# A first feed-forward layer as seven block products in two phases, with activation blocks kept in DRAM

## What is computed

```python
def conv_ffn(h, w_up, conv_w, conv_b, w_down):
    gate, val = jnp.split(dwconv_centred(h @ w_up, conv_w, conv_b), 2, axis=-1)
    return (jax.nn.silu(gate) * val) @ w_down
```

## Time and profile before

| | |
|---|---|
| median of 3 runs | 3455.32 us (3455.08 to 3456.81) |
| span of the profiled execution | 3455.1 us |
| TensorE busy | 3150.0 us, 91% |
| VectorE busy | 2289.4 us, 66% |
| GpSimd busy | 1200.4 us, 35% |
| ScalarE busy | 946.3 us, 27% |
| DMA | 196.12 MB, 57 GB/s on average |

### The profile page before, as it was taken

How to read it: one execution, slowest core, us unless ns; L and a number is a source line. 1 busy time by engine, 2 the same in 40 slices (tenths; PEclk the granted TensorE clock), 3 DMA queues, 4 the chain that set the end, 5 groups by cost and what they waited for, 6 DMA issues and landing times. The chain is left out here.

```text
span 3455.1 us, 53810 instructions
## 1 busy us (share of the span) xinstructions
PE 3150.0 (91%) x19598; PEld 2589.7 (75%) x19598; DVE 2289.4 (66%) x3256; ACT 946.3 (27%) x1512; POOL 1200.4 (35%) x1007
## 2 busy tenths in 40 slices
PE   5999989887889999999998769999998799999998
PEld 3889966665778888888886537777777577877786
DVE  8986067886366666666666436666664677777777
ACT  3111245544121111111110335554542221111111
POOL 1322145551222222222220121222121376777764
PEclk8999999998999999999999869999999899999999
DMA  4558120004011111111100200000002111111111
GB/s 195 195 191 290 68 78 2 2 2 160 31 43 37 42 42 37 36 36 37 42 30 0 83 9 10 6 5 5 5 13 80 31 49 49 55 55 49 50 48 73
DMA packets 64395, 196.12 MB, mean 57 GB/s; under 512 B 7697, under 2 KB 21009, under 8 KB 62993
## 3 DMA queue, kind: packets, MB, share of 16 engines
q1 hardware_dynamic: 47280, 163.63, 14.5%
q10 hardware_dynamic: 16992, 30.83, 2.6%
HBM read 175.56 MB, written 18.87 MB: 56 GB/s over the span
## 5 line engine op out<-in xcount | busy, mean ns | idle before, releaser
L1431 DVE SCALAR_TENSOR_TENSOR resid<-ps,mod,resid 128x256 f32<-128x256 f32 x528 | 342.0, 661 | 259.5 <-PE ps L1327 259.3
L1334 PE MATMUL ps<-hf_hi,up_hi 128*128 128x512 f32 (+1 forms) x1056 | 376.6, 357 | 17.5 <-DVE hf_lo L295 12.8
L1334 PE MATMUL ps<-hf_lo,up_hi 128*128 128x512 f32 (+1 forms) x1056 | 376.6, 357 | 0.0
L1334 PE MATMUL ps<-hf_hi,up_lo 128*128 128x512 f32 (+1 forms) x1056 | 374.8, 355 | 0.0
L1792 DVE SCALAR_TENSOR_TENSOR resid<-ps,mod,resid 128x512 f32<-128x512 f32 x352 | 255.8, 749 | 96.1 <-PE ps L1600 95.6
L1621 PE MATMUL ps<-x_hi,w_spare 128*128 128x512 f32 x824 | 290.3, 395 | 9.9 <-DVE x_lo L1717 9.2
L1302 POOL TENSOR_SCALAR up_hi<-up_raw 128x1024 fp32r<-128x1024 f32 x44 | 46.3, 1053 | 690.0 <-PE ps L1334 655.8
L837 POOL TENSOR_TENSOR k_decayed<-decay,qk 128x256 f32<-128x256 f32 (+1 forms) x240 | 193.2, 833 | 193.3 <-ACT decay L1002 193.3
L131 DVE CUSTOM_DVE_ANT_0 ps<-adaw_ring,cond,adab 128x1024 f32<-128x1024 f32 x128 | 205.8, 1608 | 55.7 <-DMA adaw_ring<-in_adaw 44.9
L1334 PEld LDWEIGHTS ps<-hf_hi,up_hi 128*128 128x128 f32 x1056 | 201.5, 191 | 44.0 <-issue 19.2
L1334 PEld LDWEIGHTS ps<-hf_hi,up_lo 128*128 128x128 f32 x1056 | 200.8, 190 | 28.6
(11 more groups left out here) (320 smaller groups left out, 8582.1 us busy)
## 6 DMA issues: line engine op xcount, KB each, us to landing
up_raw<-in_up SPq DMA_DIRECT2D x88, 512.0 KB, 3.5
adaw_ring<-in_adaw SPq DMA_DIRECT2D x80, 512.0 KB, 4.1
dn_raw<-in_dn SPq DMA_DIRECT2D x44, 512.0 KB, 3.5
vr<-vr_out ACTq DMA_DIRECT2D x80, 128.0 KB, 3.1
adaw_first<-in_adaw SPq DMA_DIRECT2D x16, 512.0 KB, 22.5
wvr_raw<-in_wvr SPq DMA_DIRECT2D x8, 1024.0 KB, 7.2
x<-in_xT ACTq DMA_DIRECT2D x8, 640.0 KB, 17.0
r<-vr ACTq DMA_DIRECT2D x10, 512.0 KB, 3.8
```

The costliest lines, as they stand in the source:

```text
L1334: mm = pe.matmul(c.psf[:, at:at + w], a[:, half, k, :], b[:, k, t:t + w], start=(k == 0 and a is up_hi and b is h_hi), stop=(k == KD - 1 a ...
L1431: dve.scalar_tensor_tensor(resid[:, m, t:t + w], c.ps[:, 6 + j % 2, 0:w], c.mod[:, gate + m, cond[t]:cond[t] + 1], resid[:, m, t:t + w], A ...
```

## The change

`ffn` and `ffn_layer` are removed, and `block_layer` with the new `block_ffn` takes their place for layer 0. With W = 640 (half of the 1280 tokens) it works in two phases.

**Start.** VectorE scales the residual in place in half-token blocks, in two parts where a block holds the 256 context tokens. ScalarE shifts the context part (`shift_context`). Then VectorE forms the differences of blocks, and for each of the seven activation blocks ScalarE writes the high part and VectorE the low part, all kept in SBUF for the phase. As this overwrites the residual, the stage before stores it to DRAM: eight 640 KB DMAs on ScalarE's queue after the squares (`spill`), with a wait for all of them at that stage's end.

**Up phase.** 22 units, one for each hidden tile. A unit is seven products of 4 k-blocks x 3 passes x 640 tokens. A region of 640 columns spans bank borders, so each pass is two matmuls, of 256 and 384 or 320 and 320 columns. Three of the seven go into a region TMP and accumulate there; ScalarE copies it out three times a unit (`move`). VectorE makes five sums of 640 columns a unit, the taps and the product. The finished activation isn't used at once: ScalarE copies it to SBUF (`keep`), VectorE forms block sums for each pair of tiles (`join`), and seven blocks of 128 x 640 for each pair are stored to DRAM.

**Down phase.** Seven products, each summed over 11 pair steps in four PSUM regions of 640 columns (4 output blocks). A step is 4 x 3 x 2 = 24 matmuls of 320 columns. For each step SyncE loads one activation block (320 KB), ScalarE makes high parts of it and of a weight block, VectorE and GpSimd the low parts, and in four of the products GpSimd also forms one weight sum per step. Ring depth is 3. VectorE adds to the residual only after a product's eleventh step (`adds`). The down weights come in four loads of 11 x 512 x 128 fp32 (2.88 MB), and the residual is loaded back, 5.24 MB.

The diff, cut to the parts spoken of (weights are also laid out anew on the host):

```diff
@@ project, ScalarE @@
                         act.activation(sq[:, s, span].unsqueeze(1), x[:, bass.ds(m, 1), span],
                                        ACT.Square).then_inc(squared, 1)
+                        if spill is not None:
+                            act.dma_start(spill[:, bass.ds(m, 1), :], x[:, bass.ds(m, 1), span]
+                                          ).then_inc(spilled, 16)
+                if spill is not None:
+                    act.wait_ge(spilled, 16 * tiles)
@@ ffn and ffn_layer @@
-def ffn(c, block, layer, h_hi, h_lo, resid, groups, seqs, wup_d, conv_d, wdn_d, out_d, ready):
...
@@ block_ffn (new) @@
+PAIRS = FT // 2
+RING = 3
+PRODUCTS = (0, 1, 2, 4, 3, 5, 6)
+DOWN = (1, 6, 0, 2, 3, 4, 5)
+TO = (("11",), ("21",), ("11",), ("21",), ("22",), ("12",), ("21", "22"))
...
+    G0, V0, TMP = (128, 1664, 3264) if W == 640 else (0, 1024, 2048)
...
+    place = (TMP, G0, TMP, G0 + W, TMP, V0 + W, V0)
+    home = [1024 * q + 192 if W == 640 else (4 + q) * BANK for q in range(HK)]
...
+    @block.sync
...
+        sp.wait_ge(block_out[1], 16 * PAIRS)
+        up_done(0)
+        for k in range(RING):
+            load(0, k, k)
+        up_done(2)
+        load_weights("12", a12, 0, 1)
+        up_done(4)
+        load_weights("22", a22, 1, 1)
+        up_done(5)
+        load_weights("11", a11, 0, 0)
+        for k in range(KD):
+            up_done(5 if k < HK else 6)
+            sp.dma_start(resid[:, k, span], spill_d[:, k, :]).then_inc(resid_in[k], 16)
+        store_value(LAST, 1, PAIRS - 1)
+        store_joined(1, PAIRS - 1)
+        for k in range(RING, PAIRS):
+            if k == 6:
+                for q in range(7):
+                    sp.wait_ge(block_out[q], 16 * PAIRS + 16)
+                load_weights("21", a21, 1, 0)
+            sp.wait_ge(d_split, k - 2)
+            load(0, k, k % RING)
...
+    @block.tensor
...
+                if pos == 1 and s:
+                    pe.wait_ge(gate_read, f * ns)
+                if pos == 2:
+                    pe.wait_ge(moved, f * 3 + 1)
+                if pos == 3 and W == 640:
+                    pe.wait_ge(mixed, f * sums_n + 1)
+                if pos == 4:
+                    pe.wait_ge(moved, f * 3 + 2)
+                if pos == 5:
+                    if s:
+                        pe.wait_ge(kept, f)
+                        pe.wait_ge(joined, f * 2 + (4 if s % 2 == 0 else 3))
...
+                for turn in ([[q] for q in spans] if pos >= 5 else [spans]):
+                    if pos == 6 and turn[0][0]:
+                        pe.wait_ge(mixed, f * sums_n + 4)
+                    for k in range(HK):
+                        if s == 0:
+                            pe.wait_ge(x_split, pos * HK + k + 1)
+                        for a, b in split_passes(w_hi[ring], w_lo[ring], x_hi[name], x_lo[name]):
+                            for at, m in turn:
+                                mm = pe.matmul(c.psf[:, place[pos] + at:place[pos] + at + m], a[:, k, :],
...
+        if W == 640:
+            for k in range(RING):
+                ready(k)
+                run(0, k, k, k, (0, 3), k == 0, False)
+            pe.wait_ge(kept, FT)
+            pe.wait_ge(joined, 4 * PAIRS + 4)
+            for k in range(RING):
+                run(0, k, k, k, (1, 2), k == 0, False).then_inc(product_done, 1)
...
+    @block.scalar
...
+        def body(act, f, s, pair):
+            if s:
+                centre_value(f - 1)
+                move(f, ua, 0)
+                keep(f - 1, (s - 1) % 2, pair)
+                move(f, ub, 2)
+            round_raw(f, s, 6)
+            act.wait_ge(mixed, f * sums_n + 1)
+            move(f, ua, 4)
...
+        for k in range(KD):
+            if ns > 1:
+                if k + 1 < KD:
+                    shift_context(k + 1)
+                act.wait_ge(shifted, k + 1)
...
+            high(k // HK, k % HK, b11 if k < HK else b21, shift_of(k))
...
+    @block.vector
...
+        def body(dve, f, s, pair):
+            if s:
+                first_value(f - 1)
+                taps(f - 1, 1)
+                product(f - 1)
+                first_gate(f)
+                join(f - 1, (s - 1) % 2, pair)
+            second_gate(f)
+            for part in range(len(value_parts) - 1):
+                second_value(f, part)
+            taps(f, 0)
+            second_value(f, len(value_parts) - 1)
...
+        dve.wait_ge(w_split, UPS)
+        for k in range(2):
+            low_step(dve, 0, k, k, k, 0)
+        first_value(LAST)
+        low_step(dve, 0, 2, 2, 2, 0)
+        taps(LAST, 1)
+        product(LAST)
+        join(LAST, 1, PAIRS - 1)
+        for k in range(RING, PAIRS):
+            low_step(dve, 0, k, k, k % RING, k // RING)
+        for q in range(1, 7):
+            down_steps(dve, q, low_step, 2, lambda: adds(q - 1))
+        adds(6)
@@ build @@
-        ffn_layer(c, a, 0, resid, 0)
+        block_layer(c, a, 0, resid, 0, BOTH_SEQ)

```

More of the change, by code:

```diff
@@ L349, in project @@
 def project(c, block, w_d, tiles, kt, x_hi, x_lo, groups, kb, evacuate, on="scalar", beside=None,
-            squares=None, ready=None, tokens=None, load_more=None, placed=None):
+            squares=None, ready=None, tokens=None, load_more=None, placed=None, spill=None):
     raw, w_hi, w_lo = placed or weight_tiles(c, kb, kt)
@@ L363, in project @@
     copied = [c.sem(f"copied{s}") for s in range(2)]
+    spilled = c.sem("spilled")
     span = slice(groups[0][0], T)
@@ L1896, in gla_layer @@
         add_projection(c, block, a["wgo"], y_hi, y_lo, resid, ALL, BOTH_SEQ, 0, 181, (resid[:, :, :], a["xT"]),
-                       c.total, tokens=tokens)
+                       c.total, tokens=tokens, spill=a["spill0"])
     return resid
 def add_projection(c, block, w_d, y_hi, y_lo, resid, groups, seqs, layer, kb, load, total, ready=None,
-                   tokens=None, placed=None):
+                   tokens=None, placed=None, spill=None):
     first = groups[0][0]
@@ L1917, in add_projection @@
     project(c, block, w_d, KD, KD, y_hi, y_lo, groups, kb, evacuate, on="vector", beside=load,
-            squares=(resid, sq, total), ready=ready, tokens=tokens, placed=placed)
-def ffn_layer(c, a, layer, resid, first, out_d=None):
-    groups, seqs = (ALL, BOTH_SEQ) if first == 0 else (LATENT, LATENT_SEQ)
-    h_hi = c.at("hf_hi", 21, [P, KD, T], F32R)
-    h_lo = c.at("hf_lo", 61, [P, KD, T], F32R)
-    with c.stage() as block:
-        ready = normalise(c, block, layer, 1, resid, h_hi, h_lo, 101, first, seqs, c.total)
-        ffn(c, block, layer, h_hi, h_lo, resid, groups, seqs, a[f"up{layer}"], a[f"conv{layer}"],
-            a[f"dn{layer}"], out_d, ready)
+            squares=(resid, sq, total), ready=ready, tokens=tokens, placed=placed, spill=spill)
 def latent_ffn(c, a, layer, resid, out_d):
@@ L1935, in latent_ffn, with block_layer @@
         seven_ffn(c, block, layer, resid, a[f"up{layer}"], a[f"conv{layer}"], a[f"dn{layer}"], out_d, holes)
+def block_layer(c, a, layer, resid, first, seqs, out_d=None):
+    with c.stage() as block:
+        block_ffn(c, block, layer, resid, first, seqs, a[f"up{layer}"], a[f"conv{layer}"], a[f"dn{layer}"],
+                  a[f"blocks{layer}"], a[f"spill{layer}"], out_d)
 KEYS = ((0, 512), (512, 512), (1024, 256))
@@ L2697, in lay_out @@
         a[f"dn{n}"] = i["ffn_w_down"][n].reshape(FT, P, D)
+    a["dn0"] = np.ascontiguousarray(
+        a["dn0"].reshape(PAIRS, 2, P, 2, BANK).transpose(3, 1, 2, 0, 4).reshape(2, 2, P, -1))
     w = i["mla_w_in"][0]
@@ L2723 @@
     drams["spill"] = nc.dram_tensor("spill", (P, KD, SEQ), F32).ap()
+    drams["spill0"] = nc.dram_tensor("spill0", (P, KD, T), F32).ap()
+    drams["blocks0"] = nc.dram_tensor("blocks0", (7, PAIRS, P, T // 2), F32).ap()
     out = nc.dram_tensor("out", (P, KD, SEQ), F32, kind="ExternalOutput").ap()
```

754 lines of the change are left out of this document (552 added, 202 removed).

## The result

| | |
|---|---|
| median after (4 runs) | 3404.17 us (3401.77 to 3405.16) |
| median before, beside it (4 runs) | 3455.93 us |
| ratio | 0.9847, 95% interval 0.9835 to 0.9859: 52 us faster |
| predicted | 3409, 3385 to 3448 |
| profiled execution of after | 3404.16 us, span 3402.4 (1.8 us lie around it) |

The page of after, as rows 1 of before: span, then busy time of each engine.

A forecast was written before the change was run, and what follows sets the result against it. TensorE's matmuls bound the stage. Its new end, 1542 + 30.6 + 274.1 + 1 + 4.2 = 1852 against 1900.4, gives -48.5; with 2 for the stores, -46.5 from 3455.1 is 3409 us, range 3385 to 3448.

The forecast's parts named there:

- The unit: Up phase: 84 passes of 640 columns take 24.6 us, with change-over 25.0 us a unit (24.6 to 25.7).
- the change-over: Up phase: time beyond the matmuls' own price in each unit, taken as 0.4 us from the old tile.
- Rival (4): Both phases: each pass pays its own excess, units 25.7 and steps 3.67, giving 3432; chance 0.09.
- rival 1: Up phase: VectorE's chain sets the unit; fully stretched, 7.4 us longer a unit, 3564; chance 0.12.
- the slack: Up phase: VectorE finishes `first_gate` at 9.1, TensorE needs it at its fourth product, 10.5: 1.4 us.
- rival 2: Down phase: GpSimd sets four of the seven products, 44 steps cost 0.4 us more each, 3427; chance 0.08.
- the rule in the prediction: VectorE with two SBUF inputs and a GpSimd instruction reading SBUF exclude each other; down phase the place to pay.
- The start: From VectorE's first scaling to unit 0's end: 64.3 us for splitting blocks plus 4.6 for the context part, 68.9.
- the shifts: Start: ScalarE's context shift in each of 8 blocks' chains, estimated at 0.45 us each; off the chain, -4.
- Between the phases: From up to down phase: idle 3.1, 7.5 and 17 plus 3 of slow clock, 30.6 us (20 to 40).
- The third gap: Ahead of down step 3: its block waits behind 16.5 MB in SyncE's queue, 17 us idle (7 to 26).
- rival (3): Between the phases: step 3's loads land before 21, so 17 and 3 us go, 3389; chance 0.11.

The follow-up runs named there:

- resid_late: Changed kernel with the residual's eight reloads issued behind the block loads of steps 6 to 9, not ahead of step 3's: 3395.23 us.
- both: Changed kernel with the edits of resid_late and experiment 2 together: 3384.11 us.
- all3: Changed kernel with the edits of both, plus the last tile's value work ahead of the second and third conversions where the phases meet: 3386.22 us.
- experiments 3 and 4: Changed kernel with one or three extra VectorE copies of a 1280-wide tile per unit, between value product and `first_gate`: 3422.97 and 3520.01 us.
- experiment 2: Changed kernel with ScalarE's high part of block k ahead of the context shift of block k + 1: 3395.59 us.
- narrow: Changed kernel with the second 320 columns of each down pass issued as 160 and 160: 3466.36 us.

## Why the prediction was right, step by step

**The unit** was 25.0 and is 24.73. The price of a matmul at 320 columns was right (0.1464 forecast, 0.147 measured); the change-over is 0.1 a unit, not 0.4. 21 x 0.27 = 5.7 us too much. Rival (4), where each pass pays its own excess, is out: units of 25.7 and steps of 3.67 it needed, 24.73 and 3.52 it got.

**The chain through VectorE** (rival 1) doesn't bind: no wait before a fourth product in after (in resid_late, both and all3 unit 1 has one of 0.9 to 1.0). But the slack was forecast at 1.4 and is 0.85. The step that is off is the wait for `centre_value`, forecast to end at 3.0: VectorE's value taps start 3.7 after a unit's end and not 3.0. So the price of one more microsecond in that chain was right in kind (21 a unit and more, experiments 3 and 4) and its point was nearer than I said. It should also have carried the clock: each gap of 3.7 us cost 2.1 more.

**GpSimd** (rival 2) sets nothing: in the steps of the down phase TensorE waits for no GpSimd instruction, and ScalarE's rounding of the weights comes every 3.52:

```profile
1607.78 0.63 ACT L2165 ACTIVATE dw_hi<-dn_a 128x512 fp32r x1 [2.25 <-PE ps L2001]
1611.30 0.63 ACT L2165 ACTIVATE dw_hi<-dn_a 128x512 fp32r x1 [2.26 <-PE ps L2001]
```

The stretching that the forecast looked for in the down phase is there, on a path that has room:

```profile
L2338 DVE TENSOR_TENSOR d_lo<-d_raw,d_hi x77: 805/1498/1975, 1540.0 to 1826.9; 128x640 fp32r<-128x640 f32 x77
```

Two of the 77 begin while GpSimd is idle and take 0.83. The other 75 begin while a GpSimd instruction runs, and 68 of them end 0.68 us after that instruction's end, however long they lasted. So here VectorE's instruction stood still until GpSimd's was over, as the rule in the prediction has it. A step has 3.52 for it.

**The start** was 68.9 and is 69.3 (unit 0 ends at 1537.9 - 21 x 24.73 = 1018.6, the first scaling is at 949.29). The sum was right and its parts were not: I gave the shifts 3.6 of it, with a lower bound of -4 for all of them; experiment 2 took 8.1 out of it by order alone.

**Between the phases** I had idle 3.1, 7.5, 17 and 3 of clock. It is 3.6, 4.8, 7.2, and the clock took more: the two groups of three half steps lasted 7.8 and 8.3 instead of 5.3, which is why the second gap is short. That clock stands after every gap and not only after the third is the step that I missed; it hid itself in the gaps behind it. The third gap is the term that was mis-sized most, 7.2 for 17. The first of the 16.5 MB went out at 1524.0 and step 3's block was in at 1568.0: 375 GB/s, where I took 350. The 47 us became 44, and the queue started 2 us earlier than the forecast's -12. Step 3 starts at 31.8 after the up phase rather than 38. It isn't rival (3), which had no third gap.

**The down phase**: steps of 3.52, not 3.56 (3 us too much over 77); each border of two products costs about 0.6 and not 0.2, 3.6 in all for 1; tail 4.3 for 4.2.

**The sum.** Stage end 1854 forecast (1852 and 2 for the stores), 1840.3 measured: 13.7 too late. Of these 6.1 lie before the end of the up phase. Between the phases I had 30.6 and it is 23.2 (31.8 to step 3 less 10.6 for three steps, and 2.0 of slow clock in step 3), 7.4 too much. In the steps, borders and tail two errors nearly cancel. Against that stand the 7.4 us in the attention stage, which no step of mine had. So 3409 for 3404.2 is nearer than its parts deserve: two errors of opposite sign, and that they cancel is luck. (On the span, which I took to be the same as the median, it is 3409 for 3402.4.)

## What to carry to other kernels

A stage that is dense on TensorE can be forecast from the distance of starts at two widths, if the new width lies between them; below them (160 columns, 0.112 against 0.080) it can't. Where a phase changes, list everything that stands ahead of the first needed load in its queue, in bytes, and move out what is needed late (5.2 MB moved, 9 us). Price a gap on a dense TensorE as itself plus the slow stretch behind it (3.7 cost 5.8 here), and look behind a changed stage too: a loop whose text is the same lost 7 us.

## What the hardware showed that I had not expected

- A wait with no releaser of 2.2 to 2.4 us at a loop's branch in a stage that the change didn't touch, with 9 packets of instructions in a pass in place of 0, and waits of 1.1 to 1.7 at the branch of the new loop. The cause is argued, not shown.
- The granted clock fell to its 1.2 GHz level behind gaps of 2.2, 3.6 and 3.7 us; behind gaps of 0.7 to 1.5 it didn't. These are no bounds: a wait of 1.96 us in the stage behind was followed by the lower level in after (0.57 over the 4 us behind it), and one of 1.95 at the same place in narrow was not (1.00).
- A low part with both inputs in SBUF ended 0.68 us behind the GpSimd instruction that ran when it began, 68 times of 77.
- A matmul of 160 columns costs 0.112 us, nearly that of 256 (0.12).
